# A decoder step on one core: the output stage starts from a tile that is still in SBUF, the sample's ranking moves to the next block, and the matmuls ahead of the dense experts are laid out anew

## The reference

```python
x1 = layer_norm(ALPHA * x + mix @ w_out)          # mix: attention and RG-LRU
q  = (x1 @ peer_wq).reshape(T, 8 heads, 2, 128)   # PEER: 16384 experts of one neuron each
sc = einsum('thpd,hpnd->thpn', q, peer_keys)      # 128 scores for each half
s1, i1 = top_k(sc[:, :, 0], 16);  s2, i2 = top_k(sc[:, :, 1], 16)
top_s, top_p = top_k(all 256 sums s1 + s2, 16);   eidx = i1 * 128 + i2 of these
g   = softmax(top_s)
ffn = sum_k g * gelu(x1 . peer_u[eidx]) * peer_v[eidx]
x2  = layer_norm(ALPHA * x1 + ffn)
y   = x2 + sigmoid(x2 @ ple_gate_w + ple_gate_b) * (p @ ple_w)
```

## Time and profile before

| | us |
|---|---|
| runs | 3714.16, 3703.18, 3712.26 (median 3712.26) |
| the profiled execution's own time | 3701.28 |
| its span | 3699.5 |
| PE busy in the span | 3407.9 (92%) |
| DVE busy | 2627.9 (71%) |
| POOL busy | 2056.1 (56%) |
| ACT busy | 840.8 (23%) |

### The profile page before, as it was taken

The page is one execution under the profiler, slowest core; times in us unless marked ns, Lnnn a source line. Parts: engine busy times, 40 slices in busy tenths (PEclk is TensorE's granted clock), DMA queues, the critical chain, the costliest instruction groups (busy, mean ns, idle before and its releaser), DMA issues.

```text
span 3699.5 us, 41566 instructions
## 1 busy us (share of the span) xinstructions
PE 3407.9 (92%) x12615; PEld 1787.6 (48%) x12615; DVE 2627.9 (71%) x5431; ACT 840.8 (23%) x1780; POOL 2056.1 (56%) x1636
## 2 busy tenths in 40 slices
PE   6999798799899987789999999999999999999878
PEld 5667463444444444644444444444444444444333
DVE  2434573348768875549888888878888788888874
ACT  1233451244343342511111111111111111111112
POOL 0000100028888888547777777777777677777630
PEclk9999899899999996699999999999999999999989
DMA  4010522478788886599999999999999999999951
GB/s 143 23 34 14 230 104 91 163 212 207 190 205 209 208 195 126 165 346 399 405 406 406 402 404 404 402 397 396 407 404 406 395 403 403 402 406 395 378 166 41
DMA packets 411333, 1025.94 MB, mean 277 GB/s; under 512 B 94045, under 2 KB 130110, under 8 KB 407554
## 3 DMA queue, kind: packets, MB, share of 16 engines
q0 software_dynamic: 221184, 604.27, 45.0%
q1 hardware_dynamic: 175858, 397.31, 30.9%
q10 hardware_dynamic: 14096, 22.02, 1.7%
HBM read 974.67 MB, written 48.77 MB: 277 GB/s over the span
## 4 chain that ended last, share of the span: by engine, by line
POOL 21%; DMA 20%; issue 8%; DVE 5%; PE 2%; ACT 0%; DVEq 0%; SPq 0%; ACTq 0%; POOLq 0%
DMA u<-in_peer_u,idx_all 20%; POOL v L2056 11%; POOL u L2048 10%; PE e_b L2199 2%; DVE facc L2092 1%; DVE u L2066 1%; DVE k_room L1998 1%; PE e_b L2187 1%; DMA wq<-in_p_prompt 0%; DMA out_y_prompt<-w_room 0%; DVE wq L2092 0%; DVE ln_st L949 0%; DVE w_room L960 0%; DVE w_room L2257 0%; DVE w_room L2230 0%
## 5 line engine op out<-in xcount | busy, mean ns | idle before, releaser
L2048 POOL DMA_INDIRECT u<-in_peer_u,idx_all x576 | 713.0, 1238 | 417.9 <-DVE act L2066 234.1
L2066 DVE CUSTOM_DVE_ANT_0 u<-u,xb 128x1024 f32<-128x1024 f32 x576 | 705.4, 1225 | 327.8 <-DMA u<-in_peer_u,idx_all 300.2
L1985 PE MATMUL e_b<-w_room,e_room 128*128 128x512 f32 x2048 | 905.6, 595 | 15.2 <-DVE k_room L1998 8.7
L1953 PE MATMUL e_b<-wq 128*128 128x512 f32 x2048 | 900.3, 592 | 0.0
L2056 POOL DMA_INDIRECT v<-in_peer_v,idx_all x576 | 702.7, 1220 | 230.5 <-issue 176.6
L1676 POOL DMA_INDIRECT gate_scratch<-e_room,slot_of x384 | 605.1, 1576 | 233.0 <-issue 116.5
L1985 PEld LDWEIGHTS e_b<-w_room,e_room 128*128 128x128 f32 x2048 | 390.4, 191 | 510.6 <-issue 490.8
L1953 PEld LDWEIGHTS e_b<-wq 128*128 128x128 f32 x2048 | 379.5, 190 | 429.0 <-issue 429.0
L2092 DVE SCALAR_TENSOR_TENSOR facc<-v,w,facc 128x1024 f32<-128x1024 f32 x317 | 406.5, 1282 | 1.4
L2092 DVE SCALAR_TENSOR_TENSOR wq<-v,w,wq 128x1024 f32<-128x1024 f32 x254 | 325.6, 1282 | 0.5
L1946 ACT ACTIVATE wq<-e_b 128x512 f32<-128x512 f32 x256 | 139.8, 594 | 724.3 <-PE e_b L1939 477.0
(11 more groups left out here) (353 smaller groups left out, 3650.9 us busy)
## 6 DMA issues: line engine op xcount, KB each, us to landing
wq<-in_peer_u SPq DMA_DIRECT2D x128, 512.0 KB
w_room<-in_peer_v SPq DMA_DIRECT2D x128, 512.0 KB
w_room<-in_cache_k SPq DMA_DIRECT2D x172, 256.0 KB
w_room<-in_cache_v SPq DMA_DIRECT2D x172, 256.0 KB
gate_scratch<-zeros SPq DMA_DIRECT2D x24, 1024.0 KB, 27.0
wq<-gate_scratch SPq DMA_DIRECT2D x96, 256.0 KB
u<-in_cache_k SPq DMA_DIRECT2D x84, 256.0 KB
u<-in_cache_v SPq DMA_DIRECT2D x84, 256.0 KB
```

Source lines behind the costliest of these rows:

```text
L1953: last = pe.matmul(AQ[c % 2][:, 0:DT], UT[c % 2][:, k, :], x1Td[:, k, :], start=(k == 0), stop=(k == KC - 1))
L1985: last = pe.matmul(OQ[i % 2][b][:], WT[n % 2][:, c, m * P:m * P + P], Vd[(4 * n + c) % NVD][:, b * 512:b * 512 + 512], start=(c == 0), sto ...
L2048: pool.indirect_dma_start(u[x % NU], None, a["peer_u"], bass.IndirectOffsetOnAxis(ap=idx_all[:, t, h, j:j + 1], axis=0)).then_inc(s_u[x % ...
L2066: dve.tensor_tensor_reduce(u[x % NU], u[x % NU], xb[t % 2][:], 1.0, 0.0, ALU.mult, ALU.add, act16[k % 2][:, j:j + 1]).then_inc(s["ufree"], 1)
```

## The change

It has four parts, all in the order and the tables of the program; the mathematics stays the same.

1. **First block, start.** The x1 tiles are turned two to a slot, at slots 0, 1, 6 and 8, the keys at slots 2 and 3, and queries start at slot 4 with two to a slot up to slot 12. All later query, score and ranking slots follow from that (last query slot 221 instead of 240, last ranking slot of batch 15 235 instead of 254).
2. **First block, end.** Quads use two PSUM banks in turn (`HOT`), stand three to a slot in slots 258 to 264 and two to a slot after, and end at slot 270; the sample's ranking is no longer in the block.
3. **Second block, start.** DVE does the sample's ranking: 4 tops before the first position, then one of the 13 remaining steps after each of positions 0 to 12. The exponential of it is ACT's at chunk 3. It works in buffers of its own (in `k_room`, which is why the first dense add waits for it). The load of `ln2_g` waits for it at chunk 16.
4. **Output stage.** The order is 3, 0, 1, 4, 5, 6, 7, 2, 8. Tile 3 is normed from its buffer in SBUF, in pieces among chunks 125 to 130, and needs no x1 or ffn row. The p product stands behind the tile's second z half for all but the last three tiles. p rows have semaphores of their own and are fetched once the turn of p has freed the buffer; the x1 row waits for y only, and the wait for the store moves to the ffn load and to the bias.

```diff
-        X_TURN, KEY_TURN, Q_FIRST = 0, 2 * UN, 12
+        X_TURN_AT = {0: (0, 1), 1: (2, 3), 6: (4, 5), 8: (6, 7)}
+        KEY_TURN_AT = {2: (0, 1), 3: (2, 3)}
+        Q_FIRST = 4
...
-        SPLIT, QUAD, NQUAD = MIXED, MIXED + 3, P // 4
+        SPLIT, NQUAD = MIXED, P // 4
+        QUAD_AT, q = {}, 0
+        while q < NQUAD:
+            x = max(QUAD_AT, default=MIXED + 1) + 1
+            n = min(3 if x <= MIXED + 8 else 2, NQUAD - q)
+            QUAD_AT[x] = range(q, q + n)
+            q += n
...
-            n = 3 if 16 <= c < 20 else 0 if c % 8 == 7 else 1
+            n = 2 if x < 12 else 3 if 16 <= c < 20 else 0 if c % 8 == 7 else 1
...
-        for e in range(NBAT + 1):
+        for e in range(NBAT):
...
-            wait(pe, s["ge"], q)
+            wait(pe, s["ge"], q - 1)
+            if q == 1:
+                pe.wait_ge(s["Oe"], DB)
             for t in range(4):
-                last = pe.matmul(B[3][:].rearrange("p (e t) -> p t e", t=4)[:, t, :], oh[q % NOH][0][:, t, :],
+                last = pe.matmul(HOT[q % 2][:].rearrange("p (e t) -> p t e", t=4)[:, t, :], oh[q % NOH][0][:, t, :],
...
+                if i == 0 and b == 0:
+                    dve.wait_ge(s["tk"], NBAT + 1)
...
-        ORDER = [t for t in range(NGT - 1)] + [t for t in range(NGT, NT)] + [NGT - 1, NT]
+        ORDER = [NGT - 1] + list(range(NGT - 2)) + list(range(NGT, NT)) + [NGT - 2, NT]
         NQ = len(ORDER)
+        BODY = NQ - 3
...
+            if q > 3:
+                sp.wait_ge(s["y"], q - 2)
+            sp.dma_start(row(q)[0:R, :], rows(x1_d, T * P, R)).then_inc(s_in[n], 16)
...
+        def first_sum_dve(dve, ch):
+            T = ORDER[0]
+            dve.wait_ge(s["vfree"], NGT * PH * TOPK)
+            ch.add(dve.scalar_tensor_tensor(out=row(0)[:], in0=row(0)[:], scalar=ALPHA, in1=facc[T % 2][:],
+                                            op0=ALU.mult, op1=ALU.add))
+            ln2.spread(dve, ch, P, row(0))
...
-        NORM_AT = {LAST - 1: 0, LAST + 1: 1}
+        SUM_AT, DEV_AT, SCALE_AT, SHIFT_AT, NORM_AT = 125, 126, 127, NCH + 2, LAST
...
-                for q in range(3, NQ):
-                    out_store(sp, q - 3)
-                    out_stored(sp, q - 3)
-                    out_load(sp, q)
-                for q in range(NQ - 3, NQ):
+                for q in range(NQ):
+                    if q + 3 < NQ:
+                        out_load_p(sp, q + 3)
                     out_store(sp, q)
...
-                out_z_pe(pe, 0, 0)
                 out_turn_p_pe(pe, 0)
                 for q in range(NQ):
-                    if q:
-                        out_z_pe(pe, q, 0)
-                    out_p_pe(pe, q)
+                    out_z_pe(pe, q, 0)
+                    if q >= BODY:
+                        out_p_pe(pe, q)
                     if q + 1 < NQ:
                         out_turn_pe(pe, q + 1)
+                    if BODY <= q < NQ - 1:
                         out_turn_p_pe(pe, q + 1)
                     if q == NQ - 3:
                         out_sample_pe(pe)
                     out_z_pe(pe, q, 1)
+                    if q < BODY:
+                        out_p_pe(pe, q)
+                        out_turn_p_pe(pe, q + 1)
...
+                        if x == 3:
+                            rank_gate_act(act, NBAT)
...
+                for name, n in RANK_STEPS[:UN]:
+                    rank_step_dve(dve, ch, NBAT, name, n)
+                rank_left = RANK_STEPS[UN:]
...
                     position(at)
+                    for name, n in rank_left[at:at + 1]:
+                        rank_step_dve(dve, ch, NBAT, name, n)
```

227 lines of the change are left out of this document (140 added, 87 removed).

## The result

The changed kernel takes 3677.10 us (median of five runs, 3667.19 to 3681.95), the kernel before beside it 3706.87 (3702.55 to 3714.16). The ratio is 0.9913, 95% interval 0.9899 to 0.9927: 32 us faster, less than the 46 that the prediction summed. The profiled execution took 3667.19, the fastest of the five, with a span of 3665.4 against 3699.5: 34.1 us less.

A forecast was written before the change was run, and what follows sets the result against it. PE bounds the second block's steady chunks, so only the first block's end, its successor's start and the output stage can give time. +5 - 42 + 8 - 17 = -46 gave 3666 us, range 3640 to 3697.

The forecast's parts named there:

- first block, start: Sixteen query steps moved ahead of slot 12 were to cost +5 us (between -5 and +16).
- first block, end: Quads in two banks, ranking moved out: -42 us (-33 to -47), -33 if the heads run at the low clock.
- second block, start: DVE ranks there: +8 us (-5 to +23.5), with 15.5 us of the ranking hidden in DVE's waits.
- output stage: PE's and DVE's waits for norms, gates and rows of p shrink: -17 us (-8 to -27).
- sequence 1 grows by 5 to 8: First block's start: 16 query steps take 12 to 15 us, and a 6.84 us wait for a page can be filled.
- The walk along PE: First block's end followed on PE from the fold at 1425 through quads, projection, LayerNorm, heads and scores to 1536.
- I put the first z at 3494.5: Output stage: the first z, behind p's turn, starts at 3494.5 instead of 3488.29; the last z ends at 3672.
- no waits over 5 us of PE in the output stage: A sign that the forecast holds: PE has no wait over 5 us in the output stage.
- The clock of the last sequence: Rival, first block: without queries, slots 222 to 239 run at 1.2 GHz, +13 us, so 3679; chance 0.14.
- Quads in a chain: Rival, first block's end: quads don't overlap and cost 4.2 us each, in sum +20, 3732; chance 0.05.
- The output stage that gives nothing: Rival: first z waits for DVE and x1 rows cost what p rows did, 3683; chance 0.07.
- the ranking paid in full: Rival, second block's start: positions don't catch up, +23.5 instead of +8, 3682; chance 0.05.

The follow-up runs named there:

- rank_back: The changed kernel with the sample's ranking back in the first block, behind the scores; ratio to the kernel before 0.9944.
- one_bank: The changed kernel with one PSUM bank for the quads again, their places kept; ratio to the kernel before 1.0049.
- out_before: The changed kernel with the output stage of the kernel before (order, loads, norms, p products); ratio to the kernel before 0.9944.
- norm_late: The changed kernel with DVE's norm of the second tile, and two positions, moved behind the last add; ratio to the kernel before 0.9910.
- p_late: The changed kernel with the first tile's turn of p moved behind its second z half on PE and ACT; ratio to the kernel before 0.9898.
- both_act: The changed kernel with the old first-block start, late first turn of p, and ACT's copy of p before the third square root; ratio to before 0.9872.
- quads_before: The changed kernel with quads as before: one bank, one to a slot from 259 to 290, ACT's old order; ratio to the kernel before 1.0018.
- one_bank_one: The changed kernel with one bank for the quads and one quad to a slot from slot 265; ratio to the kernel before 0.9970.

## Why the prediction was right and where it was wrong

The time lies in the range and on the side that was forecast, but the sum of -46 is 14 us too large. By the four moments:

| part | predicted | measured | from |
|---|---|---|---|
| first block, start | +5 | +11 | folds, 9 kernels against 4 |
| first block, end | -42 | -42 | 160.0 to 118.0, and 118.7 |
| second block, start | +8 | +9 (+11 against rank_back) | 1844.6 and 1844.1 against 1835.8; 1833.5 |
| output stage | -17 | -11 | 273.5 against 284.2 |

*First block, start* is the term that was mis-sized, and the step that failed in it is "sequence 1 grows by 5 to 8". The sixteen steps take 15 us on PE, as reckoned. The prediction let them fill the whole 6.84 us of waiting, but only what stands ahead of that page can fill the wait. One pair of the eight does, and with the turns around it 3.35 us were filled. The values of sequence 1 start 12.6 us later (13.2 by the means of the nine kernels and the four), not 5 to 8.

The return of at most 3 us in the last sequence did come, and was about right. From the start of the values of sequence 8 to the fold it is 39.2 us in all four kernels with late queries and 37.3 to 37.5 in all nine with early ones, so 1.9 us. In the kernel before it is 1382.12 to 1421.30, in the changed kernel 1393.69 to 1431.00.

*First block, end* came out to the microsecond, and some of that is luck. The prediction names the sample's ranking as what ended the block. In the kernel before, the ranking ends at 1578.35, and rank_back shows that a block which waits for it begins 0.3 us later. It began at 1581.31, behind the store and the load of the last quad: the quads were last, by some 2.6 us. For the changed kernel the prediction has 6 us of scores and 3 us of boundary behind the last head, 9 in all. Measured are 9.4, but they are SP's thirteen loads, and the scores lie beside them.

The walk along PE had a wrong detail as well. The prediction said that quads fill the norm's 5.97 us. PE waits 6.25 there, and 5.12 at the LayerNorm, because DVE makes the tiles, two quads ahead, and is itself the engine that norms. Against that the quads stood 2.04 us apart at either clock, a bit under the 2.14 taken, and the heads were as reckoned. That they were at 3.68 was luck too, since rank_back met its first two at 6.93 and 4.50. The prediction gives heads at the low clock 9 us (its -33). That is too little: in one_bank the eight heads alone cost 26 us more, which makes +50 out of some +20. The measured parts sum to -33.

*Second block, start* was right in size (15.5 of the 23.5 us of ranking hidden; 12 of 23 measured by rank_back). Against rank_back it is all paid in the first eight chunks (94.8 us from the first meet to the ninth, there 83.7). Against the kernel before only 3.3 us are lost there (91.6), and 5.6 more up to the last meet. Those 5.6 aren't the ranking's, since rank_back and out_before need them as well. Why the kernel before starts its chunks more slowly than rank_back and then runs through them faster, no run settled, so that the +9 agree with the +8 is in part chance.

*Output stage:* the step "I put the first z at 3494.5", and from there to 3672, was nearly right in its first half (in the counting of before, with the last meet 23.4 us sooner, it was 3498.0), and short in the second: 190.9 us from the first z to the end, against 187.5. Together 7 us. The sign "no waits over 5 us of PE in the output stage" failed with the 16.34. The runs norm_late, p_late and both_act show why repairing the first half brings little. In norm_late the first z comes 10 us sooner, the next bias of DVE doesn't, and PE waits 10.6 instead of 5.1 us for it. In both_act the wait moves from ACT's copy to DVE's bias. That the stage therefore runs at DVE's order of norms, biases and leftover positions is a reading of these waits. It isn't DVE's amount of work, for from the first z on DVE is busy 124 of 181 us in the changed kernel, and in the stage it itself waits 30.3 us for PE's z.

*The rivals.* The clock of the last sequence (0.14) did not come: page turns without queries ran at 1.09 us, and one stretch of 16 transposes took 3.48 us at the low clock. The prediction's own sign for it was crossed nonetheless. It asked for a clock over 0.9 between the last query and the last attention matmul. The changed kernel has 0.71 there: 0.83 up to the values of sequence 8, and 0.50 in these values, which were at 0.50 before too. The rule on transposes that the prediction takes from the Trainium skill, "TensorE: Matmul & The Clock Gate", section on "PE-mode transpose", isn't borne out by these turns of 1.09 us. Quads in a chain: one_bank has them at 2.83 even with one bank, not 4.2; that this is so because tiles are made ahead is argued, not isolated. The output stage that gives nothing and the ranking paid in full were each off by 11 or 12 us.

## What to carry to other kernels

Two pieces of work that end together at a block's end are to be priced as a pair: with the old quads the moved ranking brought nothing (quads_before is slower than the kernel before), and without the moved ranking the change is worth 11 or 12 us less. Look for the end of a block on the engine that issues loads too: here the last store and its load ended the old block and thirteen issues on SP the new one, and neither stands in a sum over PE and DVE. Before work is moved into a gap, look for what ends the gap: a page that lands at a time of its own gives room only to work that stands ahead of it, and the rest lengthens the path (16 steps moved, 3.4 us filled, 12.6 lost at the values of sequence 1, 1.9 back at the end). And where a trace has stretches that scatter more than the effect, cut it at moments that several kernels share and compare stretch by stretch.

## What the runs showed of the hardware

In these traces TensorE's clock doesn't follow from how full PE is. In one_bank PE was busy 40.5 of 45 us (90%) at a granted clock of 0.50, 1.2 GHz, with one wait of 0.78 us between the two quads of each head. In the kernel before it was busy 49.4 of 60 us (82%) at 0.93. In one_bank_one one quad stood between two heads, without a wait, and the second and third head took 4.30 and 3.68 us. In rank_back, whose work there is that of the changed kernel, the first head took 6.93 us, the changed kernel's 3.68: the same list of matmuls meets either clock. The Trainium skill, "TensorE: Matmul & The Clock Gate", section "What's actually happening", has activity release the throttle; a PE at 90% that stays at 1.2 GHz through eight heads does not agree with that sentence as it stands.
